# Compression of the prompt's own rows: operands of the first layer's matmuls exchanged, sums turned afterwards

## What is computed

```python
def nsa_compress(x, pe, w1, b1, w2):
    B, L = x.shape[:2]
    nh = L // CMP_STRIDE                       # windows of 16 tokens
    halves = x[:, :nh * CMP_STRIDE].reshape(B, nh, CMP_STRIDE, NSA_KV_HEADS, HEAD_DIM)
    first = jnp.einsum('bnskd,sdh->bnkh', halves + pe[:CMP_STRIDE, None, :], w1[:CMP_STRIDE])
    second = jnp.einsum('bnskd,sdh->bnkh', halves + pe[CMP_STRIDE:, None, :], w1[CMP_STRIDE:])
    hid = jax.nn.gelu(first[:, :-1] + second[:, 1:] + b1)
    return hid @ w2
```

## Time and profile before

| | us |
|---|---|
| median of 3 runs | 2009.44 (2008.98 to 2014.61) |
| profiled execution, device time | 2014.1 |
| its span | 2012.3 |
| busy: PE / DVE / ACT / POOL | 1832.8 / 895.4 / 677.2 / 444.4 |

### The profile page before, as it was taken

The page is one execution under the profiler, slowest core; times in us unless marked ns, Lnnn a source line. Parts: engine busy times, 40 slices in busy tenths (PEclk is TensorE's granted clock), DMA queues, the critical chain, the costliest instruction groups (busy, mean ns, idle before and its releaser), DMA issues.

```text
span 2012.3 us, 32814 instructions
## 1 busy us (share of the span) xinstructions
PE 1832.8 (91%) x13711; PEld 1661.6 (83%) x13711; DVE 895.4 (44%) x1345; ACT 677.2 (34%) x1129; POOL 444.4 (22%) x380
## 2 busy tenths in 40 slices
PE   4999997999999997999799999788876999999996
PEld 2989876999999997889678878566653999999996
DVE  6060254744434455546522422777522644444343
ACT  3243333332323233232333321666652331313130
POOL 3344224100000003433222121576812100000000
PEclk8999767999999998999898898799997999999998
DMA  4122122222222221322312110000283122222211
GB/s 158 43 84 84 45 88 88 108 102 85 84 85 84 85 89 45 106 74 95 126 53 84 43 53 1 1 1 9 91 339 149 57 113 103 107 85 85 85 43 43
DMA packets 22255, 166.28 MB, mean 83 GB/s; under 512 B 2112, under 2 KB 9840, under 8 KB 12568
## 3 DMA queue, kind: packets, MB, share of 16 engines
q1 hardware_dynamic: 17896, 122.60, 16.4%
q0 software_dynamic: 4208, 41.45, 5.5%
HBM read 154.00 MB, written 10.04 MB: 82 GB/s over the span
## 4 chain that ended last, share of the span: by engine, by line
PE 79%; DVE 9%; ACT 4%; POOL 3%; issue 2%; DMA 2%; ACTq 0%; DVEq 0%; SPq 0%; PEldq 0%; POOLq 0%
PE slot L2029 51%; PE slot L2253 11%; POOL phase L908 3%; PE slot L2240 2%; PE slot L2001 2%; PE slot L2103 1%; ACT phase L1349 1%; PE slot L2135 1%; DVE normed_x L1460 1%; PE slot L2064 1%; PE slot L2376 1%; DVE phase L1444 1%; PE slot L2436 1%; PE slot L2081 1%; DVE phase L1861 1%
## 5 line engine op out<-in xcount | busy, mean ns | idle before, releaser
L1179 ACT ACTIVATE w_high<-weights 128x1024 fp32r<-128x1024 f32 x128 | 135.3, 1060 | 258.1 <-PE slot L2029 250.0
L2029 PE MATMUL slot<-h_high,w_high 128*128 128x260 f32 x1024 | 209.6, 286 | 6.6 <-issue 6.6
L2029 PE MATMUL slot<-h_high,w_rest 128*128 128x260 f32 x1024 | 209.3, 286 | 5.6 <-issue 5.6
L2029 PE MATMUL slot<-h_rest,w_high 128*128 128x260 f32 x1024 | 208.4, 285 | 0.0
L2029 PE MATMUL slot<-u_high,w_high 128*128 128x260 f32 x1024 | 206.3, 283 | 0.0
L2029 PE MATMUL slot<-u_rest,w_high 128*128 128x260 f32 x1024 | 206.1, 283 | 0.0
L2029 PE MATMUL slot<-u_high,w_rest 128*128 128x260 f32 x1024 | 206.0, 283 | 0.0
L1640 DVE TENSOR_TENSOR w_rest<-weights,w_high 128x1024 fp32r<-128x1024 f32 x128 | 156.0, 1222 | 31.1 <-ACT w_high L1179 31.1
L2029 PEld LDWEIGHTS slot<-h_high,w_high 128*128 128x128 f32 x1024 | 160.4, 191 | 10.8 <-issue 10.5
L2029 PEld LDWEIGHTS slot<-h_high,w_rest 128*128 128x128 f32 x1024 | 160.2, 191 | 3.1 <-issue 3.1
L2029 PEld LDWEIGHTS slot<-h_rest,w_high 128*128 128x128 f32 x1024 | 160.0, 191 | 0.0
(11 more groups left out here) (354 smaller groups left out, 3780.5 us busy)
## 6 DMA issues: line engine op xcount, KB each, us to landing
weights<-in_wt SPq DMA_DIRECT2D x47, 2048.0 KB, 8.6
weights<-in_state SPq DMA_DIRECT2D x2, 2048.0 KB, 8.7
out<-weights POOLq DMA_DIRECT2D x2, 2048.0 KB, 8.7
weights<-in_w SPq DMA_DIRECT2D x2, 2048.0 KB, 9.0
phase<-in_v_win SPq DMA_DIRECT2D x4, 1024.0 KB, 6.9
out<-phase SPq DMA_DIRECT2D x6, 512.0 KB, 6.5
phase<-in_x_prompt SPq DMA_DIRECT2D x2, 1024.0 KB, 6.3
weights<-in_k_win SPq DMA_DIRECT2D x2, 1024.0 KB, 7.1
```

The source lines that it names most:

```text
L1179: nc.scalar.activation(w_part[k % 4][0][:, :, :], ring[:, s, :, 128 * (k % 4):128 * (k % 4) + 128], ACT.Copy).then_inc(w_high_ready, 1)
L2029: last = mm(ps[0:w.shape[2], a, 0:HT], w[:, k, :], m[:, k, HT * a:HT * a + HT], start=k == 0 and w is high and m is x_high, stop=k == DC - ...
```

## The change

In rounds 4 and 9 (g = 4) the operands of the first layer's matmuls are exchanged: the turned rows (128 windows and heads) become the weights of the array and w1 moves with 256 columns. That is 6 matmuls a step instead of 12, and the sums land with windows on the partitions. A new step "ht" turns them: DVE copies 128x256 out of the sums to `hid_rows`, PE transposes its two halves into the other bank of the same slot, and only then is the slot announced to ACT's GELU. For round 4 "ht" stands in round 5 after sp = 1, right before "g"; for round 9 it follows the last "m". PE's wait for its own last matmul falls away in rounds 4 and 9. Beside it some semaphores are merged (`go_high_ready` and `no_high_ready` to `heads_high_ready`, `kdt_ready` into `kt_ready`), with the counts that are waited for shifted to suit.

```diff
+        hid_rows = W(4096, 256)
...
+                    if r == 5 and sp == 1:
+                        yield "ht", 4, 0
                     if r and sp in (1, 3, 5):
                         yield from tail({1: "g", 3: "c", 5: "cn"}[sp], r - 1)
             yield "m", 9, 7
-            for what in ("g", "c"):
+            for what in ("ht", "g", "c"):
                 yield what, 9, 0
...
                     for c in range(2):
                         h2 = hid[:, c, :, :].rearrange("p m n -> p (m n)")[:, 0:rows_turned]
-                        ins_ = nc.scalar.activation(h2, ps[:, c, 0:rows_turned], ACT.Gelu_apprx_tanh,
+                        src = ps[:, c, 0:rows_turned] if g < 4 else ps[:, 1, 128 * c:128 * c + 128]
+                        ins_ = nc.scalar.activation(h2, src, ACT.Gelu_apprx_tanh,
                                                     bias=hid_bias[:, 2 * kv + c:2 * kv + c + 1])
...
+                elif what == "ht":
+                    hidden = slot[where(("hid", r))[0]]
+                    dve.wait_ge(full_mm, 8 * r + 8)
+                    if r == 9:
+                        dve.wait_ge(full[0], where(("hid", 4))[1] + 1)
+                    nc.vector.tensor_copy(hid_rows, hidden[:, 0, 0:256]).then_inc(hid_rows_ready, 1)
...
                     for half in range(2):
-                        for c in range(2):
+                        for wp, xp in ((0, 0), (0, 1), (1, 0)) if g == 4 else ():
+                            last = mm(psh[:, 0, 0:256], xt_part[xp][:, sp % 2, half:half + 128],
+                                      w1_part[wp][:, 8 * half + sp, :], start=sp == 0 and half == 0 and wp == xp,
+                                      stop=sp == 7 and half == 1 and wp == 1)
+                        for c in range(2) if g < 4 else ():
                             for wp, xp in ((0, 0), (0, 1), (1, 0)):
...
                     last.then_inc(full_mm, 1)
-                    if sp == 7:
+                    if sp == 7 and g < 4:
                         pe.wait_ge(full_mm, 8 * r + 8)
                         pe.sem_inc(fuh, 1)
+                elif what == "ht":
+                    s, k = where(("hid", r))
+                    pe.wait_ge(hid_rows_ready, kv + 1)
+                    for c in range(2):
+                        last = nc.tensor.transpose(slot[s][:, 1, 128 * c:128 * c + 128], hid_rows[:, 128 * c:128 * c + 128], ident)
+                    last.then_inc(full[s], 1)
```

More of the change, by code:

```diff
@@ L334, in trunk @@
         wgr_high_ready, wgr_rest_ready = sem("wgr_high_ready"), sem("wgr_rest_ready")
-        go_high_ready, ow_high_ready = sem("go_high_ready"), sem("ow_high_ready")
+        heads_high_ready, ow_high_ready = sem("heads_high_ready"), sem("ow_high_ready")
         go_rest_ready = {e: sem(f"go_rest_{e}") for e in ("heads", "last_head", "decode")}
@@ L338, in trunk @@
         og_last_ready = sem("og_last_ready")
-        no_high_ready, no_rest_ready = sem("no_high_ready"), sem("no_rest_ready")
+        no_rest_ready = sem("no_rest_ready")
         w_high_ready, w_rest_ready = sem("w_high_ready"), sem("w_rest_ready")
@@ L356, in trunk @@
         kp_ready = sem("kp_ready")
-        kdt_ready = sem("kdt_ready")
         at_ready = sem("at_ready")
@@ L400, in trunk @@
         kcz_ready = sem("kcz_ready")
+        hid_rows_ready = sem("hid_rows_ready")
         kc_ready = sem("kc_ready")
@@ L804, in out_rest @@
             def out_rest(h):
-                pool.wait_ge(go_high_ready, h + 1)
+                pool.wait_ge(heads_high_ready, h + 1)
                 nc.gpsimd.tensor_tensor(go_part[1][:, 2 * h:2 * h + 2, 0:NP], go[:, 2 * h:2 * h + 2, 0:NP],
@@ L1088, in out_high @@
                 nc.scalar.activation(go_part[0][:, 2 * h:2 * h + 2, 0:NP], go[:, 2 * h:2 * h + 2, 0:NP], ACT.Copy)\
-                    .then_inc(go_high_ready, 1)
+                    .then_inc(heads_high_ready, 1)
             for what, h in GLA_STEPS:
@@ L1097, in _ @@
                     nc.scalar.activation(kdt2[:, h % 2, :, :], ps[:, 0, :].rearrange("p (c k) -> p c k", c=TT),
-                                         ACT.Copy).then_inc(kdt_ready, 1)
-                    act.wait_ge(kdt_ready, h + 1)
+                                         ACT.Copy).then_inc(kt_ready, 1)
+                    act.wait_ge(kt_ready, h + 1)
                     act.sem_inc(fr, 1)
@@ L1151, in _ @@
             act.wait_ge(ogd_ready, 1)
-            nc.scalar.activation(go_part[0][:, :, NP:T], go[:, :, NP:T], ACT.Copy).then_inc(go_high_ready, 1)
+            nc.scalar.activation(go_part[0][:, :, NP:T], go[:, :, NP:T], ACT.Copy).then_inc(heads_high_ready, 1)
             act.wait_ge(og_last_ready, 1)
@@ L1391, in _ @@
                 nc.scalar.activation(kt4[m // 2 % 2][m % 2], ps.rearrange("p a n -> p (a n)"), ACT.Copy).then_inc(kt_ready, 1)
-                act.wait_ge(kt_ready, m + 1)
+                act.wait_ge(kt_ready, GH + m + 1)
                 act.sem_inc(fr, 1)
@@ L1418, in _ @@
             for c in range(DC):
-                nc.scalar.activation(no_part[0][:, c, 0:NP], no[:, c, 0:NP], ACT.Copy).then_inc(no_high_ready, 1)
+                nc.scalar.activation(no_part[0][:, c, 0:NP], no[:, c, 0:NP], ACT.Copy).then_inc(heads_high_ready, 1)
             act.wait_ge(tile_in[TILE_NSA_OUT % 2], 16 * (TILE_NSA_OUT // 2 + 1))
@@ L1425, in _ @@
             act.wait_ge(nod_ready, 1)
-            nc.scalar.activation(no_part[0][:, :, NP:T], no[:, :, NP:T], ACT.Copy).then_inc(no_high_ready, 1)
+            nc.scalar.activation(no_part[0][:, :, NP:T], no[:, :, NP:T], ACT.Copy).then_inc(heads_high_ready, 1)
             feed_forward(1, X_FF0)
@@ L1605, in _ @@
             nc.vector.tensor_tensor(go[:, :, NP:T], go[:, :, NP:T], gr[:, :, NP:T], ALU.mult).then_inc(ogd_ready, 1)
-            dve.wait_ge(go_high_ready, 4)
+            dve.wait_ge(heads_high_ready, 4)
             nc.vector.tensor_tensor(go_part[1][:, :, NP:T], go[:, :, NP:T], go_part[0][:, :, NP:T].bitcast(F32),
                                     ALU.subtract).then_inc(go_rest_ready["decode"], 1)
-            dve.wait_ge(go_high_ready, 5)
+            dve.wait_ge(heads_high_ready, 5)
             nc.vector.tensor_tensor(go_part[1][:, 2 * GH - 2:2 * GH, 0:NP], o_last,
@@ L1957, in _ @@
             for c in range(DC):
-                dve.wait_ge(no_high_ready, c + 1)
+                dve.wait_ge(heads_high_ready, GH + 1 + c + 1)
                 nc.vector.tensor_tensor(no_part[1][:, c, 0:NP], no[:, c, 0:NP], no_part[0][:, c, 0:NP].bitcast(F32),
@@ L1976, in _ @@
             dve.sem_inc(fr, 1)
-            dve.wait_ge(no_high_ready, DC + 1)
+            dve.wait_ge(heads_high_ready, GH + 1 + DC + 1)
             nc.vector.tensor_tensor(no_part[1][:, :, NP:T], no[:, :, NP:T], no_part[0][:, :, NP:T].bitcast(F32),
@@ L2107, in _ @@
                 elif what == "u":
-                    pe.wait_ge(kdt_ready, h + 1)
+                    pe.wait_ge(kt_ready, h + 1)
                     ps, fu = claim(pe, ("u", h))
@@ L2400, in _ @@
                     turn_keys(2 * n + 3)
-                pe.wait_ge(kt_ready, 2 * n + 2)
+                pe.wait_ge(kt_ready, GH + 2 * n + 2)
                 out = psw[:, 0, :] if half == 2 else psl[:, half, :]
```

## The result

The changed kernel takes 1985.5 us in the median (1982.3 to 1989.3) where the kernel before takes 2009.2; the ratio is 0.989 (95% interval 0.986 to 0.992), that is 22 us less, between 17 and 28. Its profiled execution has a span of 1980.5 us against 2012.3.

What follows compares the result with a forecast made beforehand. PE was taken to bound the kernel (busy 91%). Round 4 (7.2 - 0.4) and round 9 (6.3 - 1.0) gave 12.1 us, the clock 4.9, together 17; 15.5 off the 2009.44 median made 1994 us, range 1987 to 2004.

Steps and rivals of the forecast that it cites:

- The price of a matmul: Rounds 4 and 9: 256 columns take 0.120 us (high clock) or 0.214 (low); a step's burst saves 0.62 or 1.28.
- The formula of the skill: Issue gap is columns over the clock plus 2.5 ns: 56 ns for 128 columns, 109 for 256, so nothing gained.
- rival 3: Rounds 4 and 9: time goes by columns, so no gain, and "ht" costs 1.4 us: 2011 us; chance 0.05.
- 7.2 - 0.4 + 1.3 = 8.1 us: Round 4: 7.2 saved by bursts net of waits, 0.4 cost of "ht", 1.3 from an earlier clock rise in m(5,0).
- the 0.75 laid out: Round 4, step 6: PE waits 0.75 us for ACT's root and DVE's reciprocal, laid out at the low clock.
- the 1 us that was named as a sign of being wrong: Round 4: a PE wait of over 1 us at "ht" would show the prediction wrong.
- 6.3 - 1.0 + 2.9 = 8.2 us: Round 9: eight bursts save 6.3, uncovered "ht" costs 1.0, the high clock holding gives another 2.9.
- Rival 1: The clock gains nothing, round 9 falls to 1.2 GHz as before: 12 us less, 1997.5 us; chance 0.25.
- Rival 2: Typical runs have little low clock in rounds 4 and 9: together 6 us less, 2003.5 us; chance 0.12.
- Rival 4: Slower: PE's idle time in round 4 keeps the clock low into rounds 5 and 6: 2016 us; chance 0.03.
- rival 5: The high clock lasts into attention and gives 3 to 6 us more: 1989 us; chance 0.05.
- the 1.5 us taken off for the median: Whole kernel: 17 us for the profiled execution became 15.5, as the median run perhaps has less low clock.

Runs made afterwards that it cites:

- e3: Kernel before, but each of the 12 matmuls a step in rounds 4 and 9 moves 256 columns, the extra 128 being unread leftovers; ratio 0.994.
- e10: Kernel before with only the change's merged semaphores and 93 empty instructions at the head of PE's queue; ratio 0.996 to the kernel before.
- e1: Kernel before with the operands exchanged in round 4 alone, with its "ht", round 9 as before; ratio 0.994 to the kernel before.
- e11: Changed kernel with round 3's root and reciprocal moved to step 0 of round 5 and round 3's GELU to sp = 0; ratio 0.984 to the kernel before.

## Why the prediction was right or wrong

**The price of a matmul: right.** In the chain of round 9 a burst of six takes 0.91 us from the transposes' end, where twelve took 1.48; 0.57 less against 0.62 forecast. In order of time the new matmuls start 0.12 apart (here at the high clock, round 4):

```profile
1089.97 0.28 PE L2261 MATMUL slot<-w_high,xt_rest 128*128 128x256 f32 x1
1090.09 0.28 PE L2261 MATMUL slot<-w_rest,xt_high 128*128 128x256 f32 x1
1090.21 0.28 PE L2261 MATMUL slot<-w_high,xt_high 128*128 128x256 f32 x1
```

The prediction said that no burst with 256 columns was in the trace of before. That was an oversight: L2064, in the first layer's projections, is one, and its starts are 0.12 apart as well. The taken value held. That a load of 128 columns of weights sets the 0.112 is likely but argued only; it is no floor for every matmul, since the second layer, with 63 columns of weights and 64 moving, runs 32 in 2.05 us.

**The formula of the skill: the trace decides against it.** By columns over the clock the change would have given nothing (rival 3). e3 shows it most plainly: twice the columns at nearly the same price. The prediction also read the section too narrowly. In the Trainium skill, "TensorE: Matmul & The Clock Gate", Back-to-back issue gap, the formula is given for an isolated matmul, and the same paragraph says that it counts too little at 128 columns in a stream of weight loads and matmuls, where it has 81 ns. The 112 ns here lie above that as well, and the 232 ns at 512 columns above its 131.

**Round 4: the mechanism right, its clock mis-sized.** The forecast was 7.2 - 0.4 + 1.3 = 8.1 us, measured were 10.7. The step that failed there is the clock. It said that the clock would fall as before because PE idles ahead of the third burst, and then laid out the rest of the round at 1.2 GHz. The clock did fall at 1085.9, for the third burst and the second layer, but came back at 1089.5 and fell once more, behind the wait for the reciprocal. With fast bursts that wait is 1.55 us, not the 0.75 laid out, which gave part back; the one ahead of the third burst is 1.26 for about 1.5. Up to x(5,1) 9.2 us were saved where 7.2 were forecast, from there to x(5,3) 1.5 where 0.9 were. The prediction expected the high clock of 256-column bursts for round 9 alone, and had to carry it to round 4 as well.

**"ht": right in kind, a little dear.** In round 4, 0.26 us for 0.4; in round 9, 0.98 us from last burst to GELU for 1.1, of which 0.79 goes when it is left out. PE's idle time ahead of it in round 4 is under 0.3 us, far from the 1 us that was named as a sign of being wrong.

**Round 9: right, and its size partly by luck.** 6.3 - 1.0 + 2.9 = 8.2 us forecast, 8.0 measured; 0.7 for the second layer behind it, 0.8 measured; granted clock 1.00. The length after is steady, but the one before is not: against the 19.5 and 26.0 us of e10 and e1 the gain would be 6.7 or 13.2. Rival 1 is out by the granted clock of 1.00. Rival 2 is out because every trace with the 128-column bursts of a round has low clock in it (0.61 in round 4 of e10, 0.59 to 0.82 in round 9). Rival 4 (slower by a low clock in round 5) didn't come, as the clock was back by 1100, and rival 5 fell too: attention begins at the low clock as before (granted 0.50 in its first 7.4 us in both), and the first scores come 0.8 us sooner by the second layer alone.

**The failed step that put the time outside the range: a term left out, the place of PE's code.** What the change removes was counted in matmuls only, and not in instructions of a queue whose later loops had stops; everything behind attention was put at nothing without a reason. The runs showed 6.2 us there instead. The trace of before showed these stops (6.2 us in the second MLP, 5.9 in the first, as "issue") and the prediction named neither them nor the chance that a shift would move them. With 6.2 us beside the 19.6 the sum is 25.8, inside the measured 17 to 28. Without them it would have been 19.6, and 1990 us, inside the range; the forecast of 15.5 was short of that by round 4's clock and by the 1.5 us taken off for the median, for which the runs gave no ground.

## What to carry to other kernels

Before halving or doubling a matmul's columns, read the starts of the rows at hand: here 128 columns cost nearly what 256 cost, and the stretches with the narrow ones were granted the lower clock, for the work around them as well, so even useless columns paid. When a change takes instructions out of an engine's queue, look for "issue" gaps at the turns of later loops and at the packets of the instruction queue; here each loop that no longer stopped was worth 6 us, a few dozen empty instructions where the engine waits anyway did it, and a comparison of two kernels carries such an offset without telling.

## What the runs showed that I had not expected

- Twelve matmuls of 256 columns instead of twelve of 128 made the kernel 12.5 us faster (e3): the clock granted went from 0.61 and 0.76 to 1.00.
- 42 empty instructions made the changed kernel faster, by 13 us by the medians (1985.5 to 1972.2; the ratios are 0.989 and 0.980, with intervals that touch), and 93 of them the work of before 9 us, though an empty instruction at the head costs 0.15 us once PE's wait for its input (6.9 us) is used up.
- Moving the reciprocal out of round 4 took PE's waits out of that round and put 3.1 us of waits into the next (e11).
- The start of the kernel, up to round 4, varies between executions of the same program by 2 to 4 us, and between programs from 1071.6 to 1092.7 us; only the part that belongs to the first MLP's stops is explained.
